# Two jobs of the output projection computed inside the sample attention's block, and the projection's queue in another order

## What is computed

```
u  = LN(x) * (1 + scale1) + shift1                     # six vectors per sequence from SiLU(c) @ w_ada + b_ada
z  = u @ w_in + b_in  -> diff q,k,v | band q,k,v | gate_a | gate_b
oa = differential attention (8 heads, ALiBi, full past of 128)       # 1024 wide
ob = chunk-band attention (8 heads)                                  # 512 wide
m  = sigmoid(gate_a) * (oa @ p_a) + sigmoid(gate_b) * (ob @ p_b)
x  = LN1(alpha * x + gate1 * (m @ w_out))
u2 = LN(x) * (1 + scale2) + shift2
x  = LN2(alpha * x + gate2 * (shared SwiGLU(u2) + top-8 routed experts(u2)))   # 64 experts
```

## Time and profile before

| | |
|---|---|
| runs | 1301.11, 1299.72, 1297.0 us; median 1299.72 |
| the profiled execution | 1297.59 us, of which the span from the first to the last instruction is 1295.1 |
| PE busy | 1017.3 us, 79% of the span |
| DVE, ACT, POOL busy | 428.9, 239.2, 216.6 us |
| mean granted TensorE clock | 0.931 of full |
| block 3 | about 358 to 426 us of the span |
| block 4 | about 427 to 560 us |
| blocks 5 and 6 | from 560 us on |

### The profile page before, as it was taken

One profiled execution on the slowest core, in us unless ns is written; L12 is line 12 of the kernel. 1 busy time (PEld: TensorE's weight loads), 2 busy tenths in 40 slices (PEclk: granted clock), 3 DMA queues, 4 the chain that ended last, 5 costly groups with the idle time before them and its releaser, 6 DMA issues.

```text
span 1295.1 us, 23131 instructions
## 1 busy us (share of the span) xinstructions
PE 1017.3 (79%) x8385; PEld 652.7 (50%) x8386; DVE 428.9 (33%) x815; ACT 239.2 (18%) x478; POOL 216.6 (17%) x361
## 2 busy tenths in 40 slices
PE   4899999967675799984787777887767888746865
PEld 3898878756564344542444444444434544423432
DVE  4433343437743113875411211111111122201118
ACT  3222223335464000110110111011100111100110
POOL 0011000001300000201222222223221233312211
PEclk9899999988899799997899999899997999978988
DMA  9575535447272893066689599899999878899955
GB/s 350 174 257 186 187 130 187 162 160 257 72 245 98 296 264 114 33 286 221 219 297 392 201 403 407 335 353 348 398 380 394 314 282 344 341 407 404 388 216 228
DMA packets 96278, 347.49 MB, mean 268 GB/s; under 512 B 13425, under 2 KB 18593, under 8 KB 71514
## 3 DMA queue, kind: packets, MB, share of 16 engines
q1 hardware_dynamic: 79626, 311.55, 64.1%
q0 software_dynamic: 13856, 30.13, 6.9%
q10 hardware_dynamic: 2736, 4.98, 1.1%
HBM read 329.15 MB, written 29.52 MB: 277 GB/s over the span
## 4 chain that ended last, share of the span: by engine, by line
PE 27%; DMA 16%; issue 5%; DVE 3%; ACT 1%; SPq 0%; POOLq 0%; POOL 0%; DVEq 0%; ACTq 0%
DMA W<-w 10%; PE PS L1821 8%; PE PS L1836 7%; DMA hT<-h_rows,ixo 4%; PE PS L1852 4%; PE PS L1876 3%; PE PS L1890 2%; DMA vec<-ln_b 1%; DVE hido L1942 1%; PE PS L1810 1%; PE PS L1827 1%; PE PS L1844 1%; ACT sgo L1913 1%; PE PS L1867 0%; DVE hidTo L1945 0%
## 5 line engine op out<-in xcount | busy, mean ns | idle before, releaser
L1821 PE MATMUL PS<-W,XT 128*32 128x256 f32 x2048 | 133.2, 416 | 58.2 <-DMA W<-w 40.1
L1821 PEld LDWEIGHTS PS<-W,XT 128*32 128x32 f32 x2048 | 81.3, 120 | 124.7 <-issue 100.8
L1836 PE MATMUL PS<-W,XTo 128*64 128x256 f32 x1216 | 139.3, 381 | 0.0
L1836 PEld LDWEIGHTS PS<-W,XTo 128*64 128x64 f32 x1216 | 93.5, 137 | 42.6 <-issue 9.7
L306 PE MATMUL PS<-w_hi,u_hi 128*128 128x512 f32 x240 | 94.2, 392 | 2.3 <-DVE w_lo L432 1.8
L1852 PE MATMUL PS<-W,hidTo 128*64 128x512 f32 x304 | 80.6, 651 | 16.7 <-DVE hidTo L1945 13.7
L306 PE MATMUL PS<-w_hi,u_lo 128*128 128x512 f32 x240 | 93.4, 389 | 0.0
L306 PE MATMUL PS<-w_lo,u_hi 128*128 128x512 f32 x240 | 93.4, 389 | 0.0
L432 DVE TENSOR_TENSOR w_lo<-raw,w_hi 128x2048 fp32r<-128x2048 f32 x26 | 59.5, 2288 | 88.7 <-ACT w_hi L372 88.7
L1876 PE MATMUL PS<-W,hidT 128*32 128x512 f32 x512 | 67.6, 639 | 23.8 <-issue 19.1
L1937 DVE TENSOR_TENSOR hid<-sg,PS 64x256 f32<-64x256 f32 x32 | 19.6, 614 | 178.1 <-ACT sg L1905 175.9
(11 more groups left out here) (342 smaller groups left out, 1499.5 us busy)
## 6 DMA issues: line engine op xcount, KB each, us to landing
W<-w SPq DMA_DIRECT2D x96, 2048.0 KB, 19.2
raw<-w_in SPq DMA_DIRECT2D x26, 1024.0 KB, 5.2
wada<-w_ada SPq DMA_DIRECT2D x6, 2048.0 KB, 7.6
W<-expert_rows SPq DMA_DIRECT2D x24, 512.0 KB, 12.4
kc<-cache_k_diff SPq DMA_DIRECT2D x8, 512.0 KB, 4.8
vc<-cache_v_diff SPq DMA_DIRECT2D x8, 512.0 KB, 3.5
Wa<-p_a SPq DMA_DIRECT2D x4, 1024.0 KB, 7.3
Wa<-w_out SPq DMA_DIRECT2D x4, 1024.0 KB, 9.9
```

Of the source, the lines that this page charges most:

```text
L1821: mm = pe.matmul(PS[64 * h + 32 * c:64 * h + 32 * c + 32, UP_B + i, 0:F], XT[:, i, k, 32 * c:32 * c + 32], t.W13[:, 2 * i + c, h, k], star ...
L1836: mm = pe.matmul(PS[64 * h:64 * h + 64, XH_B, 0:F], XTo[:, k], t.W13[:, slot, h, k], start=k == 0, stop=k == KD - 1)
```

## The change

The products of jobs 0 and 1 (c = 0, tiles 0 and 1) move into block 3: job 0 behind the join matmuls, job 1 behind the last turn. They write banks 4, 5 and 6, 7, which DVE reads in block 4. Their weights are loaded in block 3 by SP, between the value loads of the last two sequences, into SBUF that held the biases and the prompt's values (one tensor `middle`, which also lends room to `W2`, `gated` and `sh_T` later). In block 4 the gates of jobs 0 to 2 are queued first, the gates of jobs 3 to 5 ahead of rows and vectors, the first half of `w_out` behind them, the second behind the vectors, the router's weights last. The waits of POOL and ACT for the first block's writes move to POOL's stream at the end of block 2.

```diff
@@ condition_and_project
+        t.written = [(mod_out[i], 64 * (MOD_Z // 2)) for i in range(2)] + [(k_out[0], 96), (k_out[1], 48), (v_out, 16 * NT * len(VC))]
+        t.written += [(g_out[i], 16 * NT * len(GC) // 2) for i in range(2)]
...
-            for i in range(2):
-                pool.wait_ge(mod_out[i], 64 * (MOD_Z // 2))
-            pool.wait_ge(k_out[0], 96)
-            pool.wait_ge(k_out[1], 48)
-            pool.wait_ge(v_out, 16 * NT * len(VC))
...
-            for i in range(2):
-                act.wait_ge(g_out[i], 16 * NT * len(GC) // 2)
@@ attention_prompt, POOL
             for i in range(2):
                 pool.wait_ge(late_out[i], 64 * len(LATE) // 2)
+            for signal, count in t.written:
+                pool.wait_ge(signal, count)
@@ attention_sample, SP
                 sp.dma_start(vc[:, b % 2, 8:12], t.cvb[b]).then_inc(vcache_in[b % 2], 16)
+                if b == NSEQ - 2:
+                    for h in range(2):
+                        sp.dma_start(t.wa0[:, 4 * h:4 * h + 4], half_of(t.p_a, h)).then_inc(t.wa0_in[h], 16)
+                    sp.dma_start(t.wb0, t.p_b[0].rearrange("(k p) n -> p k n", p=P)[:, :, 0:CW]).then_inc(t.wb0_in, 16)
@@ attention_sample, PE
                 mm.then_inc(join_mm, 1)
+            for h in range(2):
+                pe.wait_ge(t.wa0_in[h], 16)
+            pe.wait_ge(t.wb0_in, 16)
+            project_first(pe, t, 0)
             pe.wait_ge(on_done, 1)
             pe.wait_ge(sot_ev, 2)
...
                 mm.then_inc(sot_mm, 1)
+            project_first(pe, t, 1)
@@
+def project_first(pe, t, n):
+
+    q, bank = slice(P * n, P * n + P), 4 + 2 * n
+    for k in range(KD):
+        pe.matmul(t.PS[:, bank], t.oaT[:, k, q], t.wa0[:, k], start=k == 0, stop=k == KD - 1)
+    for k in range(DB // P):
+        pe.matmul(t.PS[:, bank + 1], t.obT[:, k, q], t.wb0[:, k], start=k == 0, stop=k == DB // P - 1)
@@ projection_out
-        Wa = sb("Wa", [P, 2, KD, CW])
-        Wb = sb("Wb", [P, 2, DB // P, CW])
+        Wa = [t.wa0, sb("Wa1", [P, KD, CW])[:, :, :]]
+        Wb = [t.wb0, sb("Wb1", [P, DB // P, CW])[:, :, :]]
...
-        jobs = [(c, n) for c in range(2) for n in range(NT)]
+        jobs, FIRST = [(c, n) for c in range(2) for n in range(NT)], 2
+        bank_of = lambda m: 4 + 2 * m if m < FIRST else 2 * (m % 2)
@@ projection_out, SP
+            def load_out(c):
+                sp.wait_ge(p_mm, NT * (c + 1) - FIRST)
+                sp.dma_start(Wa[c][:, 0:4], half_of(t.w_out, 2 * c)).then_inc(wa_in[c], 16)
+                sp.dma_start(Wa[c][:, 4:8], half_of(t.w_out, 2 * c + 1)).then_inc(wa2_in[c], 16)
...
+            for m in range(NT):
+                load_gates(m)
+            sp.dma_start(Wa[1][:, 0:4], half_of(t.p_a, 2)).then_inc(wa_in[1], 16)
...
+            for m in range(NT, 2 * NT):
+                sp.wait_ge(m_ev, m - NT + 1)
+                load_gates(m)
+            load_out(0)
             for n in range(2):
                 sp.dma_start(t.X[:, n], t.x_prompt[0, P * n:P * n + P]).then_inc(vec_in, 16)
...
             t.load_mod(sp, scale2, 4, vec_in)
+            load_out(1)
             sp.dma_start(t.wr[:, :, :], t.w_router[0].rearrange("(p k) e -> p k e", k=KD)).then_inc(t.wr_in, 16)
...
-            for m in range(NT, 2 * NT):
-                sp.wait_ge(m_ev, m - NT + 1)
-                load_gates(m)
-            for c in range(2):
-                sp.wait_ge(p_mm, NT * (c + 1))
...
@@ projection_out, PE (the same offset in DVE's waits)
-                if m >= 2:
+                if m >= FIRST + 2:
                     pe.wait_ge(m_ev, m - 1)
...
-            for m in range(2 * NT):
+            for m in range(FIRST, 2 * NT):
                 project(m)
@@ streaming_layer
+        biases = 2 * HA * 256
+        middle = scoped(ctx, "middle", [P, biases + NT * (DA + DB)])
...
+        t.wa0 = middle[:, 0:KD * CW].rearrange("p (k n) -> p k n", k=KD)
+        t.wb0 = middle[:, biases:biases + DB // P * CW].rearrange("p (k n) -> p k n", n=CW)
+        t.gated = middle[:, biases + DB // P * CW:biases + DB // P * CW + 2 * CW].rearrange("p (i n) -> p i n", i=2)
+        t.W2 = middle[:, 0:WB * 2 * D].rearrange("p (e j d) -> p e j d", e=WB, j=2)
```

More of the change, by code:

```diff
@@ L1177, in load_gates @@
                     sp.dma_start(G[:, m % NT, g], t.gates[2 * g + c, P * n:P * n + P]).then_inc(gt_in[m % NT], 16)
-            for c in range(2):
[L1180 to L1185, removed]
-                        load_gates(m)
+            def load_out(c):
[5 more added lines that the diff above has]
+            sp.dma_start(Wa[1][:, 0:4], half_of(t.p_a, 2)).then_inc(wa_in[1], 16)
+            sp.dma_start(Wa[1][:, 4:8], half_of(t.p_a, 3)).then_inc(wa2_in[1], 16)
+            sp.dma_start(Wb[1], t.p_b[0].rearrange("(k p) n -> p k n", p=P)[:, :, CW:2 * CW]).then_inc(wb_in[1], 16)
+            for m in range(NT, 2 * NT):
+                sp.wait_ge(m_ev, m - NT + 1)
+                load_gates(m)
+            load_out(0)
             for n in range(2):
@@ L1198, in _ @@
             sp.dma_start(r.ws13[:, :, 1], t.ws3[0].rearrange("(p k) n -> p k n", k=KD)).then_inc(r.ws_in, 16)
-            for m in range(NT, 2 * NT):
-                sp.wait_ge(m_ev, m - NT + 1)
-                load_gates(m)
-            for c in range(2):
-                sp.wait_ge(p_mm, NT * (c + 1))
-                sp.dma_start(Wa[:, c, 0:4], half_of(t.w_out, 2 * c)).then_inc(wa_in[c], 16)
-                sp.dma_start(Wa[:, c, 4:8], half_of(t.w_out, 2 * c + 1)).then_inc(wa2_in[c], 16)
             for n in range(NT):
@@ L1214, in project @@
                 c, n = jobs[m]
-                if m >= 2:
+                if m >= FIRST + 2:
                     pe.wait_ge(m_ev, m - 1)
                 q = slice(P * n, P * n + P)
-                pe.wait_ge(wa_in[c], 16)
+                if c:
+                    pe.wait_ge(wa_in[c], 16)
                 for k in range(KD):
-                    if k == 4:
+                    if c and k == 4:
                         pe.wait_ge(wa2_in[c], 16)
-                    pe.matmul(PS[:, 2 * (m % 2)], t.oaT[:, k, q], Wa[:, c, k], start=k == 0, stop=k == KD - 1)
-                pe.wait_ge(wb_in[c], 16)
+                    pe.matmul(PS[:, bank_of(m)], t.oaT[:, k, q], Wa[c][:, k], start=k == 0, stop=k == KD - 1)
+                if c:
+                    pe.wait_ge(wb_in[c], 16)
                 for k in range(DB // P):
-                    mm = pe.matmul(PS[:, 2 * (m % 2) + 1], t.obT[:, k, q], Wb[:, c, k], start=k == 0, stop=k == DB // P - 1)
+                    mm = pe.matmul(PS[:, bank_of(m) + 1], t.obT[:, k, q], Wb[c][:, k], start=k == 0, stop=k == DB // P - 1)
                 mm.then_inc(p_mm, 1)
@@ L1443, in routing @@
         none, place, dest = sb("none", [P, NBLK]), sb("place", [P, NBLK]), sb("dest_r", [P, NBLK], I32)
-        sh_g, sh_h, sh_T = sb("sh_g", [P, 2, F]), sb("sh_h", [P, NT, F]), sb("sh_T", [P, 2, 2, P])
+        sh_g, sh_h, sh_T = sb("sh_g", [P, 2, F]), sb("sh_h", [P, NT, F]), t.turned_shared
         mask_done, rank_mm, cnt_mm, code_done, list_mm = (sem(x) for x in
```

23 lines of the change are left out of this document (13 added, 10 removed).

## The result

The changed kernel takes 1295.41 us (median of 20 runs, 1282.21 to 1302.74), the kernel before, beside it, 1302.51 us (20 runs, 1297.0 to 1307.01): a ratio of 0.9937, 95% interval 0.9922 to 0.9952, or 8.2 us less. The forecast was 17.2 us less. The ratio leaves out three runs that count as slow because they lie over 1.5% above the fastest (1301.49, 1302.17 and 1302.74 us; the median of the other seventeen is 1294.34), and the profiled execution is the last of these.

The account below looks back on a forecast made before the run. PE was taken as the chain, with a hole before job 0, and SP's full queue second; 18.2 - 0.5 + 1.05 - 3.5 + 1.9 = 17.2 us saved gave 1282.5 us, range 1276 to 1288.5.

Parts of the forecast that it names:

- Two jobs in the hole: Jobs 0 and 1 fill PE's idle at the attention block's end, so job 2 starts at once: 18.2 us saved.
- The margin of the values: Last value loads, queued behind 3.15 MB of weights, land 0.2 us before PE wants them: 0.5 us lost, ends 0 and 2.3.
- The stall takes the clock with it: Rival: a 6 to 7 us wait or missed `Wa[1]` loses 5 to 6 more, giving 1287.5 us; chance 0.18.
- `w_out` behind the vectors: First output job: PE waits 3.9 us for `w_out`'s second half instead of 0.38; 3.5 us lost, ends 0 and 19.
- the 27.5 us read off `wr`: Time the rows and vectors take in SP's queue, from the landing of the 7.86 MB ahead to 477.1.
- The rival in which they drain in time: Vectors in SP's queue take 23.6 us or less instead of 27.5, no new stall: 1279.0 us; chance 0.27.
- the estimate of 19 us: Time for all vectors by the engine-count rule (8 engines for the sample's `mod` rows); `w_out` would be in time.
- Gates first, `Wa[1]` hidden: Six gate loads stand ahead of `Wa[1]`, whose load stays hidden from job 3 by 1.2 to 2.7 us.
- The turn: PE's first turn of `M` no longer waits, as gates of jobs 3 to 5 land by 456: 1.05 us saved.
- the first boundary: Waits removed at the first block's end let the next block start sooner: 1.9 us saved, ends 0.8 and 2.2.
- slower: Rival: `w_out`'s second half lands at 508, 21 late; 23.5 us lost with the clock, 1302.5 us; chance 0.03.
- the address changes: `W2`, `sh_T` and `gated` only change their address: nothing gained or lost.

Follow-up runs that it names:

- e1: The changed kernel run again as it is, beside the kernel before: 1296.2 us, ratio 0.9945 to the kernel before.
- e11: The changed kernel unchanged, in another group beside the kernel before: 1292.64 us, ratio 0.9952 to the kernel before.
- e2: Changed kernel with the three weight loads (3.15 MB) behind the last sequence's values instead of ahead: 1291.63 us, ratio 0.9925 to the kernel before.
- e10: Changed kernel with only `p_b` moved behind the last value loads, awaited before job 0's second half: 1289.18 us, ratio 0.9922 to the kernel before.
- e9: Changed kernel whose second output part starts on the first half of its `w_out` columns: 1287.81 us, ratio 0.9903 to the kernel before.
- e8: Changed kernel, weights behind last values, `shift2`/`scale2` behind `w_out`, plus `Wa[1]` ahead of gates of jobs 1 and 2: 1281.34 us, ratio 0.9851 to the kernel before.
- e5: Kernel before with only ACT's and POOL's waits on the first block's writes moved: 1299.51 us, ratio 0.9987 to the kernel before.
- e6: Changed kernel with the hole filled but SP's queue in its old order: 1310.5 us, ratio 1.0073 to the kernel before.
- e4: Changed kernel with weights behind the last values and `shift2`, `scale2` behind `w_out`'s second half: 1282.75 us, ratio 0.9852 to the kernel before.
- e7: Repeat on another chip: changed kernel with weights behind the last values and `shift2`, `scale2` behind `w_out`: 1281.43 us, ratio 0.9846 to the kernel before.
- e3: Changed kernel with `shift2` and `scale2` behind `w_out`'s second half, on their own semaphore: 1286.51 us, ratio 0.9881 to the kernel before.

## Why the prediction was wrong, point by point

Its direction was right, its size twice too large: 17.2 us less were forecast, a ratio of 0.987, 8.2 were measured, 0.9937, and 1295.4 lies beyond the range's upper end of 1288.5. Two terms of the sum failed, each with the clock behind it, and a third a little.

- **Two jobs in the hole, 18.2 saved**: right. Job 0 to job 2 takes 23.2 us, forecast 23.1, and 23.2 in e1 and e11 too.
- **The margin of the values, 0.5 lost**: this step failed first. Measured 6.8 in the first trace, 3.6 of wait and 3.2 of clock, 5.9 in e1 and 5.8 in e11. The formula put 390 GB/s on everything in the queue, from end to end, also on the values. The load of 392.62 should have brought the last values by 407.1 by it; they came at 410.97. By the windows 1.5 us of that are the first six microseconds, at 269, 258 and 353 GB/s instead of 390 (0.58 MB short), the rest is the slow end of the last value load, from 408 on. Why its last packets come so late isn't shown. The forecast kept 2.3 as the other end for the wait and nothing for the clock. A margin of 0.2 worked out with the weights' steady rate is no margin; e2 removes the wait, and its trace is 3.2 to 4.5 us ahead of those of the changed kernel in "between".
- **A short stall does not cost its own length alone.** "The stall takes the clock with it" had a chance of 0.18 and was set against waits of 6 to 7. The runs show the clock fallen behind waits for the values of 2.9 to 4.6 (each time to 0.50), and in e10 of 1.65. The forecast's reason against it, "only waits well above 3.9 are at stake, in the midst of dense matmuls", is refuted: e9's wait for `w_out` was 3.31, between dense matmuls, and the clock fell within a microsecond of its end. That rival came true in part: in the changed kernel's three traces the waits for `w_out` were 4.8 to 7.0, with 2.1 to 3.0 of clock behind them.
- **`w_out` behind the vectors, 3.5 lost**: right in its mechanism and in the vectors, wrong in one count. The vectors were forecast to land 51.4 us after the block's first load (488.2 - 436.8), and landed 51.3 after it (493.83 - 442.49); in the five other traces with this order of the queue it is 50.5 (e11) to 55.5 (e10), 52.7 in e1. The whole agrees with the sum that held the 27.5 us read off `wr`; how it divides was not measured, and the first half of `Wa[1]` was 2.7 us late in it. The rival in which they drain in time needed 3.9 less and falls. With it falls the estimate of 19 us from the rule of the Trainium skill's page "DMA: Bandwidth & Descriptors", section "Why a DMA increments its semaphore by 16 and not by 1": the trace has the half share that fits that rule (0.54 from 482 to 486), but also 165 GB/s at a share of 1.01 from 474 to 478, so that there the number of engines at work is not what limits the rows. The failed count: the sum let PE start on the first 1.05 MB of `w_out`, the code waits for both halves before the first matmul. That is 2.7 us, and e9, which makes PE wait by half, starts it 2.5 instead of 5.3 behind the vectors. Measured cost of the term: 7.0 (4.6 of wait, 2.3 of clock), 8.7 in e1 and 7.5 in e11.
- **Gates first, `Wa[1]` hidden by 1.2 to 2.7**: missed. Job 3 waits 0.6 to 2.3 us in all traces with the filled hole but that of e8. The sum again had 390 GB/s from 2.4 us after the first issue; 446 to 450 shows 265. The windows behind this point and the one before (the columns as above):

```profile
446.00:450.00 4.00, 4.00 (x11) 1.79 (x10) 2.20 (x3) 0.00 (x0) 0.00 (x0) 1.00 0.82 265
...
474.00:478.00 4.00, 4.00 (x16) 2.16 (x15) 1.92 (x2) 1.08 (x2) 0.00 (x0) 1.00 1.01 165
...
482.00:486.00 4.00, 4.00 (x11) 1.78 (x10) 0.00 (x0) 0.00 (x0) 0.00 (x0) 1.00 0.54 190
```

- **The turn, 1.05 saved**, and **the first boundary, 1.9 saved**: right (0 and 0.42 left; e5 shows the latter alone).
- **The rival "slower"** (an endless wait of `w_out`) didn't come. e6 shows that this change did have a slower side: with the queue in the old order it loses 9.5 us, a good part of it at the values. The forecast named the reordered gates for 1.05 us, when without them the first term would have been worth nothing. The hole and the queue are one gain, not two.
- **The gain of the repairs**: with both late transfers mended the kernel saves 19 to 20 us, which is the forecast's sum without its two losses: 18.2 + 1.05 + 1.9 = 21.2, less the small waits before jobs 0 and 3, which come to 3.1 in e4, 1.0 in e7 and 0.95 in e8. That the address changes cost nothing is the one term that no run settles (see above).

Still open is why the changed kernel's runs spread from 1282 to 1303 us, twice as wide as those of before, when e4, e7 and e8, with five or six runs each, stay within 5 to 7 us. The time goes with the mean granted clock of the run: in e1 three runs of 1285 to 1287 us had 0.936 to 0.941, six of 1296 to 1300 had 0.926 to 0.932. That a wait takes the clock with it in some executions and not in others would fit; so would a clock that varies in the experts' blocks. Each trace shows one execution.

## What to carry to other kernels

When work is moved into a hole, the queue that feeds what comes after must be shortened by as much, or the hole only moves (e6). Put each load behind what is wanted before it, by the order in which PE and DVE ask, and count everything that one wait asks for, with the rates that the trace shows for that transfer, its end included. In this kernel a stall of 1.65 to 8.7 us in front of PE cost its own length and 1.3 to 3.9 us more for the clock, and the extra did not grow with the length. Removing one stall is worth less than it cost where the next load in line becomes the one that is waited for (of the 6.5 us that e3 lost at the values, e4 got back 4.4).

## What the runs showed of the hardware

- The granted clock fell to its lower level, 0.50 (1.2 GHz), inside waits of PE of 1.65, 2.9, 3.0, 3.7, 3.8, 4.5 and 4.6 us at the end of the attention's block, and inside waits of 4.8 to 8.7 us between dense matmuls, or just behind one of 3.3. The work behind a wait of 4.5 us was 3.2 us slower, behind 2.9 us 3.9 slower, behind 1.65 us 1.3 slower; between dense matmuls it was 1.7 to 3.0 us slower. After 1.65 us the clock was back before the join, after 4.5 us it was still down in it.
- Transfers of the same queue differ: windows full of weights show 391 to 407 GB/s while `p_a` and `p_b` pass and 351 to 391 while `w_out` passes, those among the rows of `mod` 165 GB/s at a full DMA share and 190 at a share of 0.54.
- The last value load behind 3.15 MB of weights had a slow end: a DMA share of 0.05 to 0.18 for the last 2.5 us of it.
